# Up projection: 14 of the 22 gate and up pairs taken two at a time by seven block products

## The reference

```
h = rmsnorm(h_res, norm_ffn_w) * (1 + sc_f) + sh_f     # 512 tokens x 1024
u = h @ w_up                                           # 512 x 5632
u = causal depthwise conv of width 3 over tokens + conv_b
gate, up = split(u)                                    # 2816 each
out = (silu(gate) * up) @ w_down
```

## Time and profile before

| what | us |
|---|---|
| median of three runs | 871.58 (871.32 to 872.28) |
| profiled execution | 871.48 |
| its span | 869.7 |
| TensorE busy | 855.4 (98%) |
| VectorE busy | 607.9 (70%) |
| ScalarE busy | 487.5 (56%) |
| GpSimd busy | 251.8 (29%) |
| up projection, from the first interleaved matmul to the end of unit 44 | about 518 to 758 |

### The profile page before, as it was taken

One profiled execution on the slowest core, in us unless ns is written; L12 is line 12 of the kernel. 1 busy time (PEld: TensorE's weight loads), 2 busy tenths in 40 slices (PEclk: granted clock), 3 DMA queues, 4 the chain that ended last, 5 costly groups with the idle time before them and its releaser, 6 DMA issues.

```text
span 869.7 us, 12717 instructions
## 1 busy us (share of the span) xinstructions
PE 855.4 (98%) x4688; PEld 709.2 (82%) x4688; DVE 607.9 (70%) x779; ACT 487.5 (56%) x739; POOL 251.8 (29%) x227
## 2 busy tenths in 40 slices
PE   7999999999999999999999999999999999999996
PEld 6778878887888888888887888888888888888885
DVE  4599988678967867765955466744444444599995
ACT  5576555677558657665756444533333333357574
POOL 2124779624112131231344000211111111534200
PEclk9999999999999999999999999999999999999999
DMA  9996487283544545445325731533333336599912
GB/s 336 359 334 144 100 205 102 73 270 90 170 148 119 158 137 166 126 142 169 87 61 192 155 90 49 146 97 96 96 96 96 96 96 229 116 268 206 232 38 97
DMA packets 149235, 130.21 MB, mean 150 GB/s; under 512 B 4743, under 2 KB 132065, under 8 KB 148928
## 3 DMA queue, kind: packets, MB, share of 16 engines
q1 hardware_dynamic: 136048, 110.84, 41.5%
q0 software_dynamic: 13136, 18.69, 12.8%
HBM read 125.31 MB, written 4.20 MB: 149 GB/s over the span
## 4 chain that ended last, share of the span: by engine, by line
PE 74%; ACT 1%; DVE 1%; issue 0%; ACTq 0%
PE ps L2221 18%; PE ps L2223 17%; PE ps L2222 17%; PE ps L2653 4%; PE ps L2654 4%; PE ps L2652 4%; PE ps L2388 1%; PE ps L2543 1%; PE ps L2544 1%; PE ps L2547 1%; PE ps L2390 1%; PE ps L2368 1%; PE ps L2352 1%; PE ps L2355 1%; PE ps L2400 0%; PE ps L2337 0%
## 5 line engine op out<-in xcount | busy, mean ns | idle before, releaser
L2221 PE MATMUL ps<-h_hi,w_hi 128*128 128x512 f32 (+1 forms) x568 | 223.3, 393 | 0.5 <-DVE w_lo L1853 0.5
L2223 PE MATMUL ps<-h_lo,w_hi 128*128 128x512 f32 (+1 forms) x568 | 219.4, 386 | 0.0
L2222 PE MATMUL ps<-h_hi,w_lo 128*128 128x512 f32 (+1 forms) x568 | 219.4, 386 | 0.0
L2221 PEld LDWEIGHTS ps<-h_hi,w_hi 128*128 128x128 f32 x568 | 106.7, 188 | 23.1 <-issue 1.0
L2222 PEld LDWEIGHTS ps<-h_hi,w_lo 128*128 128x128 f32 x568 | 106.7, 188 | 22.3 <-issue 1.0
L2223 PEld LDWEIGHTS ps<-h_lo,w_hi 128*128 128x128 f32 x568 | 106.7, 188 | 21.6
L984 POOL TENSOR_TENSOR prod<-conv 128x512 f32 x21 | 43.4, 2065 | 219.7 <-DVE conv L2063 219.7
L1385 ACT ACTIVATE conv<-ps,vecs 128x512 f32<-128x512 f32 x42 | 32.6, 778 | 132.6 <-PE ps L2223 124.1
L2059 DVE SCALAR_TENSOR_TENSOR conv<-ps,vecs,conv 128x511 f32<-128x511 f32 x44 | 32.9, 749 | 104.9 <-ACT conv L1385 102.5
L1853 DVE TENSOR_TENSOR w_lo<-raw,w_hi 128x1024 fp32r<-128x1024 f32 x46 | 58.3, 1281 | 55.0 <-ACT w_hi L1026 54.9
L1512 DVE TENSOR_TENSOR w_lo<-raw,w_hi 128x1024 fp32r<-128x1024 f32 x52 | 64.3, 1239 | 0.9 <-ACT w_hi L1018 0.8
(11 more groups left out here) (312 smaller groups left out, 1814.2 us busy)
## 6 DMA issues: line engine op xcount, KB each, us to landing
raw<-in_w_in_dram SPq DMA_DIRECT2D x44, 512.0 KB, 3.8
raw<-in_w_up_dram SPq DMA_DIRECT2D x44, 512.0 KB, 3.6
ada_w<-in_w_ada_dram SPq DMA_DIRECT2D x32, 512.0 KB, 4.5
ada_w<-in_w_ada_dram SPq DMA_DIRECT2D x8, 1024.0 KB, 10.5
g_blocks<-in_w_in_dram SPq DMA_DIRECT2D x24, 256.0 KB, 6.2
hres<-in_w_down_dram POOLq DMA_DIRECT2D x12, 512.0 KB, 8.8
raw<-in_w_down_dram SPq DMA_DIRECT2D x11, 512.0 KB, 5.9
raw<-in_w_out_dram SPq DMA_DIRECT2D x8, 512.0 KB, 5.2
```

The costliest lines, as they stand in the source:

```text
L2221: pe.matmul(dst, a_hi, b_hi, start=start and i == 0, stop=False)
L2222: pe.matmul(dst, a_lo, b_hi, start=False, stop=False)
L2223: last = pe.matmul(dst, a_hi, b_lo, start=False, stop=stop and i == n - 1)
```

## The change

Four pairs stay as before (8 units, now straight code), then come seven "duos" of two pairs, then four pairs as before. In a duo the product of a 1024 x 256 weight block (gate and up of two pairs: two times 256 columns) with 1024 x 512 of h is cut in 2 x 2 x 2 blocks: k in two halves of 512, tokens in two halves of 256, gate and up as the two sides. Instead of eight block products there are seven (M1 to M7), each of 2 column tiles x 4 k-tiles x 3 matmuls with 256 moving columns. Their left sides are weights or sums of weights, their right sides blocks or sums of blocks of h:

- M5, M6, M4 take sums of weight blocks that grow in one tile `sum_tile(d)`: `first_sum` is an addition on GpSimd (128x1024), `second_sum` and `fourth_sum` are transfers from DRAM that add into the tile, each released by the low part that last read it. M7 takes `b12_tile(d)` after the accumulating `third_sum`. M1, M3, M2 take plain blocks from two tiles used in turn (`ring_tile`).
- The order on TensorE is M5(d), M4(d-1), M1(d), M3(d), M6(d), M2(d), M7(d). Seven `w_hi`/`w_lo` slots' worth per duo go through the same ring of six; each high part is made in the step of the product six before.
- The products add up in PSUM. Four intermediate values are copied out by ScalarE (`keep`: y1, x1, u1, u2), and VectorE makes three combinations per duo in PSUM (c12, c11, c22). The taps of duo d-1 are spread over the products of duo d.
- The four sums of blocks of h are made once on GpSimd (`h_sum`), from a second float32 copy of h that ScalarE writes in the norm; their high and low parts follow on ScalarE and VectorE.
- One block of h is saved to DRAM and brought back for the tail. The loads of `fw_b` and `gf_b` and of the first weights of the down projection move to the end of the duos.

The core of the diff:

```diff
+AHEAD_PAIRS, DUOS = 4, 7
+TAIL_PAIRS = FT - AHEAD_PAIRS - 2 * DUOS
+M1, M2, M3, M4, M5, M6, M7 = range(7)
+DUO_SEQ = [(p, e) for d in range(DUOS) for p, e in ((M5, d), (M4, d - 1), (M1, d), (M3, d), (M6, d), (M2, d), (M7, d))
+           if e >= 0] + [(M4, DUOS - 1)]
+U_DUO = U_UP + 2 * AHEAD_PAIRS
+U_TAIL = U_DUO + len(DUO_SEQ)
+U_DOWN = U_TAIL + 2 * TAIL_PAIRS
+LAST_DUO = DUOS - 1
+H_HALF, T_HALF = KT // 2, T // 2
+RING_ORDER = (M1, M3, M2)
...
+                act.activation(prod[:, KT + k], n_tmp[:, k % 2], ACT.Identity, bias=ada[:, 24 + k:25 + k]
+                               ).then_inc(n_hi_made, 1)
...
+            def b12_load(d):
+                if d >= 2:
+                    sp.wait_ge(lo_made, duo_at(M7, d - 2) + 1)
+                elif d == 1:
+                    sp.wait_ge(lo_made, U_DUO)
+                else:
                     sp.wait_ge(m_lo_made, M_LO[-1])
+                sp.dma_start(b12_tile(d), up_rows(0, d, 1)).then_inc(b12_in[d % 2], 16)
+            def ring_load(n):
+                d = n // 3
+                if n >= 2:
+                    sp.wait_ge(lo_made, ring_unit(n - 2) + 1)
+                elif n == 1:
+                    sp.wait_ge(lo_made, U_DUO - 2)
+                if n % 3 == 2:
+                    sp.wait_ge(*first_made(d))
+                k_half, side = ((0, 0), (1, 1), (1, 0))[n % 3]
+                sp.dma_start(ring_tile(n), up_rows(k_half, d, side)).then_inc(ring_in[n % 2], 16)
+            for d in range(DUOS):
+                b12_load(d)
+                ring_load(3 * d)
+                ring_load(3 * d + 1)
+                if d == 0:
+                    sp.wait_ge(*h2_made(KT - 1))
+                    sp.dma_start(h21_dram, h_block(0, 1)).then_inc(h21_moved, 16)
+                ring_load(3 * d + 2)
...
+            def first_sum(d):
+                pool.wait_ge(*b12_loaded(d))
+                pool.wait_ge(*ring_loaded(3 * d))
+                if d >= 2:
+                    pool.wait_ge(lo_made, duo_at(M4, d - 2) + 1)
+                elif d == 1:
+                    pool.wait_ge(lo_made, U_DUO - 1)
+                else:
+                    pool.wait_ge(n_lo_made, KT)
+                pool.tensor_tensor(sum_tile(d), b12_tile(d), ring_tile(3 * d), ALU.add).then_inc(w1_made, 1)
+            def third_sum(d):
+                pool.wait_ge(*first_made(d))
+                pool.dma_start(b12_tile(d), up_rows(1, d, 1), accum_op=ALU.add).then_inc(w3_added[d % 2], 16)
+            def second_sum(d):
+                pool.wait_ge(lo_made, duo_at(M5, d) + 1)
+                pool.dma_start(sum_tile(d), up_rows(1, d, 1), accum_op=ALU.add).then_inc(w_added[d % 2], 16)
+            def fourth_sum(d):
+                pool.wait_ge(lo_made, duo_at(M6, d) + 1)
+                pool.dma_start(sum_tile(d), up_rows(1, d, 0), accum_op=ALU.add).then_inc(w_added[d % 2], 16)
...
+            pool.wait_ge(*h2_made(KT - 1))
+            h_sum(0, s_full[0], h_block(1, 1), h_block(0, 1), ALU.subtract, 0)
+            first_sum(0)
+            third_sum(0)
+            h_sum(1, s_full[1], h_block(0, 0), s_full[0], ALU.add, 1)
+            gated_pair(0, 0, 1)
+            second_sum(0)
+            h_sum(2, s_full[2], s_full[1], h_block(1, 0), ALU.subtract, 2)
+            gated_pair(1, 2, 3)
+            pool.wait_ge(*h21_out)
+            h_sum(3, s_full[3], h_block(0, 0), h_block(0, 1), ALU.subtract, 3)
+            for pair in range(2, AHEAD_PAIRS):
+                gated_pair(pair, 2 * pair, 2 * pair + 1)
+            for d in range(DUOS):
+                fourth_sum(d)
+                if d + 1 < DUOS:
+                    first_sum(d + 1)
+                    third_sum(d + 1)
+                if d >= 2:
+                    gated_duo(d - 2, 0)
+                    gated_duo(d - 2, 1)
+                if d + 1 < DUOS:
+                    second_sum(d + 1)
+            gated_duo(LAST_DUO - 1, 0)
+            gated_duo(LAST_DUO - 1, 1)
...
+            def duo_hi(p, d):
+                u = duo_at(p, d)
+                if p == M5:
+                    act.wait_ge(*first_made(d))
+                elif p == M6:
+                    act.wait_ge(*second_made(d))
+                elif p == M4:
+                    act.wait_ge(*fourth_made(d))
+                elif p == M7:
+                    act.wait_ge(*third_made(d))
+                else:
+                    n = 3 * d + RING_ORDER.index(p)
+                    act.wait_ge(*ring_loaded(n))
+                act.wait_ge(proj_done, u - RING + 1)
+                act.activation(ring_quarter(w_hi, u), duo_source(p, d), ACT.Copy).then_inc(hi_made, 1)
...
+            for m in range(2 * AHEAD_PAIRS):
+                act.wait_ge(proj_done, U_UP + m + 1)
+                conv_unit(m)
+                if m % 2:
+                    silu_unit(m - 1)
+                if m == 3:
+                    act.wait_ge(ht_done, TT)
+                    sum_hi(0)
+                if m == 5:
+                    sum_hi(1)
+                    sum_hi(2)
+                if m == 7:
+                    sum_hi(3)
+                next_hi(U_UP + m + RING)
...
+            for i, (p, d) in enumerate(DUO_SEQ):
+                u = U_DUO + i
+                act.wait_ge(proj_done, u + 1)
+                if p == M5:
+                    if d >= 2:
+                        act.wait_ge(*c22_made(d - 2))
+                    keep(y1_tile(d), y_of(d))
+                elif p == M1:
+                    if d >= 2:
+                        act.wait_ge(*c11_made(d - 2))
+                    keep(x1_tile(d), x_of(d))
+                elif p == M6:
+                    if d:
+                        act.wait_ge(*c12_made(d - 1))
+                    keep(u1_tile, x_of(d))
+                elif p == M7:
+                    if d:
+                        act.wait_ge(*c22_made(d - 1))
+                    keep(u2_kept[:], x_of(d))
+                    if d == LAST_DUO:
+                        act.wait_ge(*h21_in)
+                        act.activation(h_part(h_hi, 0, 1), quarter(p0[:]), ACT.Copy).then_inc(s_hi, 1)
+                next_hi(u + RING)
+                if p == M5 and d >= 2:
+                    silu_unit(conv_duo(d - 2) + 3)
+                elif p == M3 and d:
+                    act.wait_ge(*c22_made(d - 1))
+                    conv_unit(conv_duo(d - 1))
+                elif p == M6 and d:
+                    conv_unit(conv_duo(d - 1) + 1)
+                elif p == M2 and d:
+                    act.wait_ge(*c11_made(d - 1))
+                    conv_unit(conv_duo(d - 1) + 2)
+                elif p == M7 and d:
+                    conv_unit(conv_duo(d - 1) + 3)
+                    silu_unit(conv_duo(d - 1) + 2)
...
+            for i, (p, d) in enumerate(DUO_SEQ):
+                u = U_DUO + i
+                if p == M4:
+                    dve.wait_ge(proj_done, u + 1)
+                    dve.wait_ge(*x1_kept(d))
+                    dve.tensor_tensor(c11_of(d), x1_tile(d), z_of(d), ALU.add).then_inc(corner, 1)
+                    dve.wait_ge(*u2_taken(d))
+                    dve.wait_ge(*c11_made(d))
+                    dve.scalar_tensor_tensor(out=z_of(d), in0=u2_kept[:], scalar=-1.0, in1=y1_tile(d),
+                                             op0=ALU.mult, op1=ALU.subtract).then_inc(corner, 1)
+                next_lo(u + RING)
+                if p == M2:
+                    dve.wait_ge(proj_done, u + 1)
+                    dve.wait_ge(*u1_kept(d))
+                    dve.scalar_tensor_tensor(out=y_of(d), in0=y_of(d), scalar=-1.0, in1=u1_tile,
+                                             op0=ALU.mult, op1=ALU.subtract).then_inc(corner, 1)
+                if p in (M3, M6, M2, M7) and d:
+                    taps(conv_duo(d - 1) + (M3, M6, M2, M7).index(p))
...
+            def duo_unit(p, d):
+                u = duo_at(p, d)
+                pe.wait_ge(lo_made, u + 1)
+                if p == M5:
+                    pe.wait_ge(conv_made, max(convs_before(up_bank(d) + i, conv_duo(d)) for i in range(2)))
+                    pe.wait_ge(*sum_low(0))
+                elif p == M1:
+                    pe.wait_ge(conv_made, max(convs_before(gate_bank(d) + i, conv_duo(d)) for i in range(2)))
+                elif p == M3:
+                    pe.wait_ge(*y1_kept(d))
+                    pe.wait_ge(*sum_low(2))
+                elif p == M6:
+                    pe.wait_ge(*x1_kept(d))
+                elif p == M7:
+                    pe.wait_ge(*u1_kept(d))
+                    pe.wait_ge(*sum_low(3))
+                elif p == M4:
+                    pe.wait_ge(*u2_taken(d))
+                dst = y_of(d) if p in (M5, M3) else z_of(d) if p == M2 else x_of(d)
+                a_hi, a_lo = duo_moving(p)
+                b_hi, b_lo = ring_quarter(w_hi, u), ring_quarter(w_lo, u)
+                more = p not in (M5, M1, M2)
+                for i in range(2):
+                    ch = slice(i * P, (i + 1) * P)
```

(53 more changed lines are left out.)

384 lines of the change are left out of this document (287 added, 97 removed).

## The result

The changed kernel takes 876.48 us (median of 5 runs, 875.61 to 878.16); in the same series the kernel before took 871.61 us (5 runs, 871.32 to 873.77). The ratio is 1.0055, 95% interval 1.0038 to 1.0073: slower, where 865.3 us and faster were predicted. The profiled execution took 875.61 us, 4.1 more than that of before (871.48); both have about 1.8 us around the span. I account for these 4.1 us.

A forecast was written before the change was run, and what follows sets the result against it. The prediction took the up projection to be bounded by TensorE's matmul columns alone. It summed 871.5 - 11.6 (matmuls) + 1.5 (circle) + 2.4 (start) + 1.5 (boundaries) = 865.3 us, range 860 to 879.

The forecast's parts named there:

- the start: Entry to the duos: fourth_sum(0) and first_sum(1) queue behind pair 3's gate product on GpSimd; TensorE stalls 2.4 us at M6(0).
- token sums: Sums of h on GpSimd beside the eight leading units, and ScalarE's second write of h: hidden, no cost.
- Matmuls: Up projection: 1176 matmuls of 256 columns at 0.1197 us replace 672 of 512 at 0.2267, gain 11.6 us.
- the circle: Weight sums through GpSimd and reused tiles, closing once a duo: 20.9 us a turn against TensorE's 20.1, stall 1.5 us.
- the boundaries: Other new waits at the 49 product boundaries, on low parts and PSUM banks: 1.5 us together (0 to 7).
- Tail: Last four pairs in the old form, transfers shared with six down-projection weight loads: 0 us, up to 3.
- DMA share: Busy share of the DMA engines during the duos, expected near 0.8 between 565 and 705 us.
- Many small stalls: Rival: VectorE, at 84%, late 0.15 to 0.2 us at each product boundary, 7 to 10 us; 869 to 874, chance 0.15.
- The slower rival: ScalarE standing at hi M6(d+1) for second_sum makes a turn up to 25.3 us; 872 to 885 us, chance 0.23.

The follow-up runs named there:

- e2: Changed kernel with fourth_sum(0), first_sum(1) and third_sum(1) put ahead of the gate product of pair 3 on GpSimd: 874.59 us, 1.0020 of the kernel before.
- e1: Changed kernel with the second and third sum of h moved on GpSimd to right behind the first: 870.39 us, 0.9977 of the kernel before.
- e5: Changed kernel with the moves of e1 and e2 together: 867.89 us, 0.9945 of the kernel before.
- e7: e5 with eight duos instead of seven and a tail of two pairs instead of four: 873.61 us, 1.0013 of the kernel before.
- e4: Changed kernel with 60 extra matmuls of 256 columns, results unread, ahead of M3(0): 876.73 us, 1.0057 of the kernel before.
- e6: Changed kernel with the first three sums of h on VectorE instead of GpSimd and the order of e2: 866.44 us, 0.9932 of the kernel before.

## Why the prediction was wrong

The mechanism of the gain was right and its size too; one step of the losses failed, "the start", and with it the zero that stood for the token sums.

- **Matmuls**: 11.6 us predicted. The pitch is 0.12 us (600.04 to 602.92 in 0.12 steps), and the account closes with 11.6 to within 0.5. Right.
- **The start**: predicted 2.4 us, measured 9.7 us of waits (7.64 and 2.04) and 3.8 of low clock behind them. This is the step that failed. It said "ScalarE and VectorE have it by 565": TensorE was indeed done with the leading units at 562.65, but VectorE reached their last tap at 574.7, since its low parts had taken 2.38, 3.94 and 7.52 us where I had 1.22. The rest of that step was sized well: from the product's start to M6(0) I had 8.6 us (565 to 573.6), measured 7.5 (575.63 to 583.14). e2 takes this chain out of the way and keeps the first wait; e1 takes most of the port's part out and leaves this chain, 4.0 us instead of 2.4; e5 takes both, down to 1.0.
- **Token sums**: "run on GpSimd beside the eight leading units", cost nothing. I looked at whether GpSimd has the time for them and not at what they do to VectorE, though the earlier trace rows showed the mutual slowdown and I used it for the circle and the boundaries. The bound "a sum can hold up a low part by 2.6 us" was also too low: 2.6 us is one instruction, and GpSimd had three queued; one alone held a low part up by 2.9 us (4.10 instead of 1.21, e5).
- **The circle**: predicted 1.5 us, measured none in the changed kernel. The prices were too high: issue 1.3 us (taken 1.8), landing 6.1 median for second_sum (7.5), first_sum 2.9 median (3.2). ScalarE's copies took 0.58 to 0.60 (0.78). The lower end of the turn adds up to 17.1 us, not 17.4, and a gate product of the earlier trace rows ends 1.15 us behind the low part, not 1.28; neither bears on the sum.
- **Boundaries**: predicted 1.5, measured 1.6 (0.76 and 0.84). The size is luck: not a little at each of 49, but two waits for taps that stand behind low parts of over 3 us.
- **Tail**: 0 predicted and, in the changed kernel, no wait of TensorE behind 721 us. e7 shows that this holds for four pairs and not for two.
- **DMA share**: 0.8 predicted between 565 and 705 us, 0.84 measured (0.87 between 600 and 700).

Of the rivals, none was it. "Many small stalls" had the right engine (VectorE) in the wrong form: not 49 small waits but one backlog at the entry. The slower rival had the wrong place; that its times (872 to 885) hold the 876.48 is luck. What the profile of before could have told: VectorE was to get four more low parts and GpSimd four sums in the 43.5 us that hold the leading units, and the earlier trace rows showed that each holds up the other.

Open: how the 13.4 us of the start divide into wait and clock as causes. e4 shows that the first slow stretch is hidden behind GpSimd's chain; for the second I have no run. The block products of e5 and e6 begin about 1 us later than those of the changed kernel (563.65 and 563.88 against 562.65; e1 began at 562.10). That has nothing to do with the changes: TensorE's 101st matmul, far ahead of any line that they touch, starts at 13.94 and 14.04 us there and at 12.79 in the changed kernel.

## What to carry to other kernels

Work put on an "idle" GpSimd holds up VectorE's instructions with two inputs in SBUF for as long as GpSimd has such instructions queued without a gap; lay the two engines' queues side by side before you call it hidden. A held instruction counts as busy, so a high busy share of VectorE may be waiting. When a stage is entered with less slack than the one before had, look for backlog at the entry, not for the steady pace: here seven duos ran well and the first twenty microseconds lost the whole gain. And when a wait is removed, look up which chain ends next, for it may end only a few microseconds earlier (e1, e4).

## What the runs showed of the hardware

- A low part of 128x1024 with both inputs in SBUF took 7.52 us beside three GpSimd instructions in a row (7.51 in e2), 3.94 beside two, and 1.22 where two of the three were short. Beside a single first_sum one took 4.10 us (e5), although by the record it started 0.08 us before it (starts on GpSimd are rough). The other way round GpSimd's first_sum took 2.40 us once and 2.82 to 3.45 six times in the changed kernel. VectorE's taps, with one operand in PSUM, kept 0.73 to 0.75 us everywhere.
- The granted clock went to its lower level (1.2 GHz) while TensorE stood for 7.5 us, and 256 columns were then 0.21 us apart instead of 0.12. The number of slow starts behind a wait doesn't follow its length: 22 behind 7.5 us (changed kernel), 17 behind 8.0 (e2), 26 and 17 behind about 4 (e1, e4), 17 behind the second wait of 1.9 (changed kernel). Behind 1.0 us (e5) the clock stayed at 1.00, and only the first start was late, 0.19 us.
- An accumulating transfer of 512 rows of 1 KB took GpSimd 1.3 us to issue, little more than the 1.2 us for 256 rows; so the price does not follow the rows as I had extrapolated.
